# Four sums of the hidden activations on another engine, and one copy placed one step earlier, in an encoder layer of fp32 products in three passes

## The reference

```python
proj = u @ w_in                       # the last 2048 columns are the gates
g = sigmoid(gates + b_gate)           # g.reshape(b, s, 2, D)
merged = g[:, :, 0] * y_conv + g[:, :, 1] * y_attn
m = merged @ w_o
h = h + rmsnorm(m, g1)
u = rmsnorm(h, g2)
f = square(relu(u @ w_ff1)) @ w_ff2   # 1024 -> 4096 -> 1024
h = h + rmsnorm(f, g3)
```

## Time and profile before

| | |
|---|---|
| median of 3 runs | 1377.79 us (1377.33 to 1377.92) |
| the profiled execution | 1378.19 us |
| its span, first to last instruction | 1376.4 us |
| TensorE busy | 1367.0 us, 99% |
| VectorE busy | 981.2 us, 71% |
| ScalarE busy | 587.6 us, 43% |
| GpSimd busy | 109.5 us, 8% |
| mean granted TensorE clock | 1.000 |

### The profile page before, as it was taken

One profiled execution on the slowest core, in us unless ns is written; L12 is line 12 of the kernel. 1 busy time (PEld: TensorE's weight loads), 2 busy tenths in 40 slices (PEclk: granted clock), 3 DMA queues, 4 the chain that ended last, 5 costly groups with the idle time before them and its releaser, 6 DMA issues.

```text
span 1376.4 us, 17472 instructions
## 1 busy us (share of the span) xinstructions
PE 1367.0 (99%) x6377; PEld 1120.6 (81%) x6377; DVE 981.2 (71%) x1415; ACT 587.6 (43%) x907; POOL 109.5 (8%) x73
## 2 busy tenths in 40 slices
PE   9999999999999999999999999999999999999998
PEld 8778778778778888888888888888888888888886
DVE  7786886885989664667376886777664786765676
ACT  7443543543545454511243453333333444444453
POOL 0000000000000000000000333233333000000000
PEclk9999999999999999999999999999999999999999
DMA  5101111101111332445721354444445973345342
GB/s 188 47 27 33 35 30 30 46 15 46 30 31 61 100 126 99 146 147 170 253 82 57 107 182 148 161 153 146 153 146 212 358 270 110 98 125 191 113 130 108
DMA packets 141646, 162.04 MB, mean 118 GB/s; under 512 B 6861, under 2 KB 88970, under 8 KB 141450
## 3 DMA queue, kind: packets, MB, share of 16 engines
q1 hardware_dynamic: 135568, 148.27, 33.3%
q10 hardware_dynamic: 6010, 12.88, 2.4%
HBM read 114.98 MB, written 46.14 MB: 117 GB/s over the span
## 4 chain that ended last, share of the span: by engine, by line
PE 63%; DVE 1%; DMA 0%; ACT 0%; issue 0%; ACTq 0%; DVEq 0%
PE psum L1012 25%; PE psum L1166 21%; PE psum L886 13%; PE psum L1143 3%; PE psum L1115 1%; DVE v L2331 0%; DMA gates_scratch<-staging 0%; DVE y L2346 0%; ACT staging L1319 0%; DVE op L2213 0%; DVE op L2210 0%; DVE f_out L2190 0%; DVE prod L1947 0%; DVE f_out L2188 0%; DVE norms L2320 0%
## 5 line engine op out<-in xcount | busy, mean ns | idle before, releaser
L1166 PE MATMUL psum<-op 128*128 128x512 f32 x1344 | 305.1, 390 | 0.5 <-DVE op L2213 0.5
L1166 PEld LDWEIGHTS psum<-op 128*128 128x128 f32 x1344 | 252.3, 188 | 53.2 <-issue 0.9
L886 PE MATMUL psum<-act_hi,w_hi 128*128 128x512 f32 x448 | 178.9, 399 | 1.0 <-DVE act_lo L1719 1.0
L886 PE MATMUL psum<-act_hi,w_lo 128*128 128x512 f32 x448 | 175.1, 391 | 0.0
L886 PE MATMUL psum<-act_lo,w_hi 128*128 128x512 f32 x448 | 174.7, 390 | 0.0
L2210 DVE TENSOR_TENSOR op<-v,op 128x512 fp32r<-128x512 f32 x112 | 78.6, 702 | 89.2 <-ACT op L1580 89.2
L1580 ACT ACTIVATE op<-v 128x512 fp32r<-128x512 f32 x112 | 70.7, 632 | 151.5 <-PE psum L1166 147.3
L886 PEld LDWEIGHTS psum<-act_hi,w_hi 128*128 128x128 f32 x448 | 84.2, 188 | 19.2 <-DVE w_lo L1725 1.6
L886 PEld LDWEIGHTS psum<-act_hi,w_lo 128*128 128x128 f32 x448 | 84.1, 188 | 18.0
L886 PEld LDWEIGHTS psum<-act_lo,w_hi 128*128 128x128 f32 x448 | 84.4, 188 | 16.3
L1819 DVE CUSTOM_DVE_ANT_0 e<-psum,alibi 128x1024 f32<-128x1024 f32 x64 | 78.1, 1221 | 11.0 <-issue 10.6
(11 more groups left out here) (271 smaller groups left out, 2808.3 us busy)
## 6 DMA issues: line engine op xcount, KB each, us to landing
f_raw<-f_scratch SPq DMA_DIRECT2D x112, 256.0 KB, 2.7
w_raw<-in_w_in SPq DMA_DIRECT2D x34, 512.0 KB, 4.6
w_raw<-in_w_ff SPq DMA_DIRECT2D x32, 512.0 KB, 4.9
f_scratch<-f_out SPq DMA_DIRECT2D x56, 256.0 KB, 2.3
v<-in_w_ff SPq DMA_DIRECT2D x12, 1024.0 KB, 8.1
gates_scratch<-staging ACTq DMA_DIRECT2D x32, 256.0 KB, 2.0
gate_in<-gates_scratch SPq DMA_DIRECT2D x16, 512.0 KB, 4.3
f_scratch<-staging SPq DMA_DIRECT2D x30, 256.0 KB, 2.2
```

The costliest lines, as they stand in the source:

```text
L886: mm = nc.tensor.matmul(bank, stat(a, kt), moving(b, kt), start=(n == 0), stop=(n == len(terms) - 1))
L1166: mm = nc.tensor.matmul(psum[:, (X_BANK, Z_BANK)[m % 2][t]], op[n % SLOTS][:, 2 + a, token_cols(t)], op[n % SLOTS][:, b], start=(m in (0, ...
```

## The change

Two edits. In the feed-forward block, GpSimd forms the sums S3, S1, S2, S4 for pairs 0 to 14 only. For pair 15 VectorE forms them, one behind each of the splits of steps 2, 3, 4 and 5. SyncE's stores of pair 15's S3, S1, S2, F12 and S4, which stood around the load of step 5, stand behind the loads of steps 6 to 9. In the gates, for pairs 3 to 6, ScalarE's copy behind X2(p) stands ahead of the tanh of C11(p); it stood behind it.

```diff
@@ SyncE
             sp.wait_ge(mix_done, FF1.at("X4", p))
             f_load(SLOTS)
-            keep("S3", p)
             f_load(SLOTS + 1)
-            for name in ("S1", "S2", "F12", "S4"):
-                keep(name, p)
...
             for n in range(SLOTS + 2, Y_STEPS):
                 f_load(n)
+
+                for name in {6: ("S3",), 7: ("S1",), 8: ("S2", "F12"), 9: ("S4",)}.get(n, ()):
+                    keep(name, PAIRS - 1)
@@ GpSimd
             pool.wait_ge(u2_ready, TT)
-            for p in range(PAIRS):
+            for p in range(PAIRS - 1):
@@ ScalarE, gates
+                if p > GATE.first:
+                    x_copy(GATE, 2, p)
                 gate_block("C11", p)
                 if p > GATE.first:
-                    x_copy(GATE, 2, p)
                     gate_block("C21", p - 1)
                 g_part_hi("W12", p + 1)
                 g_part_hi("W22", p)
@@ VectorE
+            def last_f_sum(k):
+
+                p = PAIRS - 1
+                name, a, b, op = (("S3", "F11", "F21", ALU.subtract), ("S1", "F21", "F22", ALU.add),
+                                  ("S2", "S1", "F11", ALU.subtract), ("S4", "F12", "S2", ALU.subtract))[k]
+
+                dve.wait_ge(f_sums, 4 * p + k)
+                if name == "S3":
+                    f_made(dve, "F11", p)
+                    f_made(dve, "F21", p)
+                    dve.wait_ge(f_kept["S3"], 16 * p)
+                elif name == "S1":
+                    f_made(dve, "F22", p)
+                elif name == "S2":
+                    dve.wait_ge(f_kept["F11"], 16 * (p + 1))
+                else:
+                    f_made(dve, "F12", p)
+                    dve.wait_ge(f_kept["S4"], 16 * p)
+                vec.tensor_tensor(f_block(name, p), f_block(a, p), f_block(b, p), op).then_inc(f_sums, 1)
...
             for n in range(2, Y_STEPS):
                 step_lo(n)
                 m, k = divmod(n, STEPS)
+                if n < 6:
+                    last_f_sum(n - 2)
```

## The result

The changed kernel takes 1379.73 us (median of 22 runs, 1378.78 to 1380.21), the kernel before 1377.80 (22 runs, 1377.27 to 1378.22). The ratio is 1.0014, 95% interval 1.0008 to 1.0020: 1.9 us slower. That is less than 0.2%, but it goes the other way than the forecast of 1376.45 and lies 1.8 us above the end of its range. The runs spread a little wider too, over 1.4 us where it was 1.0. Of all runs in this document one, of sums_first_pair, took 1710.27 us at a mean granted clock of 0.752; the ratios leave it out. The profiled execution is the fastest of the 22, 1378.78 us, with a span of 1377.1.

A forecast was written before the change was run, and what follows sets the result against it. TensorE, busy 99% of the span at full clock, bounds the kernel, so only its waits give time: 1377.79 less 1.34 (0.54 at X3(3), 0.80 at step 2) makes 1376.45 us, range 1375.9 to 1377.9.

The forecast's parts named there:

- the delay of Z2(6): In the gates, Z2(6) late if C11(6)'s store is slow: up to 0.8 us, taken as zero, 0.8 kept for the range.
- the 3.82 us that the prediction took as its bound: Longest gate store cited, with weight loads in flight; used as upper limit for C11(6)'s store.
- the prediction's own chain: Gates, pair 6: copy, tanh of C11, its store, tanh of C21, W12(7)'s split, VectorE's sum of C22(6), then Z2(6).
- 0.9 is in hand: In the gates, sum of C22(6) ends at 552.9 and Z2(6) needs it at 553.84, so 0.9 us spare.
- The reserve of 0.4 us at X4(7): In the gates, if C22(6)'s store is slow too, X4(7) still has some 0.4 us left.
- Rival (b): Gain partly given back: Z2(6) or X4(7) up to 0.8 late, or 0.54 soaked up; 1376.9 to 1377.25 us, chance 0.20.
- rival (d): Slower: C11 stores over about 4.1 us in pairs 4 to 6 stall X4(p); 1380.6 with 5.5 us stores; chance 0.03.
- The sizes of the two stalls: TensorE loses 0.80 us at step 2 of the second feed-forward product and 0.54 at X3(3) in the gates; 1.34 together.
- The mechanism of edit 1: VectorE's splits near step 2 are slow only beside GpSimd's sums; moving those to VectorE regains 0.80 us.
- rival (c): Full DMA engines, not GpSimd, slow VectorE: step 2 stays 0.80 late, 1377.25 us, or up to 1381.6; chance 0.05.
- (e): Something the trace does not show, such as instruction placement or DMA interleaving, moves the time 1 us or more; chance 0.06.

The follow-up runs named there:

- sums_first_pair: The changed kernel, but with the copy ahead of the tanh for pair 3 alone: 1377.15 us, ratio 0.9996 to the kernel before.
- after_third_buffer: The changed kernel, but C21(5)'s tanh writes to an idle tile, so it needs no wait for C11(6)'s store: 1377.12 us, ratio 0.9996 to the kernel before.
- sums_only: The kernel before with only pair 15's sums moved to VectorE with their stores, gates unchanged: 1377.60 us, ratio 0.9999 to the kernel before.

## Why the prediction was wrong

**The step that failed** is the one on edit 2 that took zero for the delay of Z2(6): "I take zero, since at 544 to 547 no load is in flight in either kernel". It priced the store of C11(6) at 2.15 us from C11(3)'s. The store held the tanh for 3.6 to 4.6 us. No load was in flight, but an instruction packet was, which I had not looked for. The page of the kernel before lists that queue, its trace has the packet at 545.4, 1.6 us behind the place to which the store was moved, and it even has a slow store there, that of C21(5), issued at 544.40. DMA view of the kernel before, 543 to 549:

```profile
q8 instruction: 1, 0.02, 1.8%
...
gates_scratch<-staging ACTq DMA_DIRECT2D x1, 256.0 KB, 4.3
```

Nothing waits for that store in the kernel before, so it is on no chain; yet it is slower than the 3.82 us that the prediction took as its bound. The change put in its place a store that something waits for.

The delay follows the prediction's own chain: 3.55 in place of 2.15 makes the sum of C22(6) 1.4 us late, 0.9 is in hand, and TensorE waits 0.43 us and loses 0.67 between starts. The reserve of 0.4 us at X4(7) failed too: C22(6)'s store took 4.44 us where 3.82 was the bound, and it started late besides. Rival (b), chance 0.20, named the right two places, Z2(6) and X4(7), and the wrong size: up to 0.8, where the two lost 1.59 in the fastest execution and the wait for C11(6)'s store is worth 2.6 to 2.9 in the medians. Its bound was the slowest store on the chain of before, 3.82 us, and it let only one of two late stores count. They are in series: the late first one delays the second, which is slow among the loads in any case (4.1 us even in after_third_buffer), and X4(7) loses on top of Z2(6). From 4.11 us on, the place of rival (d), X4(6), begins to pay too; (d) asked for three late pairs and had its threshold of 4.1 right.

**What held.** The sizes of the two stalls: X3(3) starts at 488.02, forecast 488.01, and step 2 has no gap. The mechanism of edit 1: without GpSimd the splits take 0.68 us, with the DMA engines as full (a share of 1.04 in 1064 to 1084, as before), so rival (c) falls. The four sums are hidden behind TensorE, one per step. Copy and tanh of pair 6 were forecast at 542.6 and 543.1 and stand at 542.62 and 543.11.

**What was left out.** 0.36 us at the end, in front of one VectorE operation, which the prediction had only under (e), without a price. And the medians of the clean versions, 1377.12 and 1377.15, lie some 0.6 us below before, where 1.34 - 0.36 = 0.98 is expected from the profile; sums_only shows the same, 0.12 for 0.44. Where the other 0.3 to 0.4 us went is open. The profiled execution of before was 0.4 us above its median, so its stalls may have been larger than usual; a second profile of it was not taken.

## What to carry to other kernels

When an instruction is moved ahead of others in one engine's order, follow what it now holds back to the first wait on a DMA landing, and ask for that landing not the usual time but the time beside everything in flight, instruction packets too. Look at what lands at that time in the trace of before, waited for or not: the store of 4.3 us was there. Compare it with the smallest reserve downstream, and add late landings that are in series. A copy that is ready pays nothing for being moved up; one that waits holds everything behind it, so here only the first pair was worth moving. A tile of its own for the one tanh that waited took the landing off the path, and the spread between runs fell from 1.4 us to 0.5.

## What the runs showed of the hardware that I had not expected

A 256 KB store from ScalarE's queue held the next tanh for 2.15 us when the DMA engines were otherwise idle. The same store held it for 3.6 to 4.6 us with one 16 KB instruction packet among its packets, and 2.15 again when that packet was moved. Over all profiles such a meeting made a landing take 2.8 to 4.5 us, in place of 2.01 to 2.07. The store of C11(3) agrees: its waiter started 2.15 us after the issue in the kernel before, with the packet at 489.46, behind it, and 3.0 us after in the changed kernel, with the packet at 487.63.

Of waits that are always met only a part become instructions in the profile: 20 on TensorE added 5 or 10, 40 on VectorE added 20. And the four sums with their waits, 9 more instructions in VectorE's stream, brought a delay of 0.36 us to an operation 300 us later; 20 more at the start of the stream took it away.
